# Reordered waits in a two-layer hybrid trunk: gate scans, attention scores, filler jobs and their evictions change places

## The chip, the core and the metric

The kernel runs on one core of a Trainium2 chip. The metric is device time of one execution in microseconds (us). Engines are named TensorE (PE), VectorE (DVE), ScalarE (ACT), GpSimd (POOL) and SyncE (SP).

## What is computed

Two trunk layers are applied to a prompt of 128 tokens and to a sample of 256 tokens with cached context, at width 1024, in float32. The reference, cut to what matters:

```python
h = rms_norm(x, norm1_w) * (1 + scale1) + shift1
(mq, mk, mv, mo, mg, nq, nk, nv, dq, dk, dv, sz, sxbc, sdt, gpre) = split_cols(h @ w_in)   # 1024 x 7448
a_out = mlstm_mixer(...)      # gated linear attention, forward and backward
b_out = na_mixer(...)         # neighbourhood attention, 4 heads
c_out = diff_mixer(...)       # p0 - lam * p1 from two softmaxes, 4 heads
d_out = ssm_mixer(...)        # 5-tap convolution, then a decaying scan, forward and backward
gates = sigmoid(gpre)         # 4 x 1024 columns
mixed = sum(gates * (branches @ w_branch))
x = x + gate1 * (mixed @ w_out)
x = x + gate2 * expert_choice_ffn(rms_norm(x, norm2_w) * (1 + scale2) + shift2, ...)       # 16 experts
```

## The kernel before, in words

The 384 tokens are three tiles (TT) of 128. Each layer has the same stages, written out by hand engine by engine, with semaphores between them. Each engine works its own list in order, so an instruction that waits holds up all that stand behind it.

1. **Projections.** Seven weight tiles (PROJ_TILES) are multiplied in three passes: each weight quarter is split by ACT (high_parts: rounding copy into a four-slot ring, line 1368) and by POOL (low_parts: difference, line 710), and PE does 24 matmuls per quarter (three_passes, line 769). Between them PE turns the gate rows: line 871 waits for rows_ready, which DVE signals after the gate scans (lines 1860 to 1872). DVE does, in this order: norm of the neighbourhood queries and keys (nan_ready), the 20 steps of the convolution (lines 1843, 1845, conv_ready), the gate scans (rows_ready).
2. **Filler jobs.** The 32 gate quarters (g0 to g31; 24 matmuls each), the 8 modulation partials (p0 to p7; 16 matmuls, line 775) and their sums (s0 to s7; 8 matmuls, line 781) are 48 jobs in the order JOB_ORDER. PE runs them between the small matmuls of the mixers. They alternate between banks 0 and 1: a job waits until the one two before it is evicted by take_job on ACT (line 1513, tanh, or 1368, copy). take_job also starts a store of the previous gate and then splits weights of later quarters (high_parts(AHEAD[j])).
3. **Neighbourhood attention** (ten units). PE: a job, na_scores(i), na_turn(i-1), na_out(i-2). DVE: na_in (scale, bias, maximum), na_take. ACT: na_exp (waits for o_evac of unit i-2, since the sum SSUM has two places), take_job, na_turned.
4. **Differential attention** (twelve units). PE: df_scores(i), a job, df_turn(i-1), df_out(i-2). DVE: df_max(i), df_mix(i-1), df_take(i-2). After the last df_out DVE normalises the result (head_norm) and only then turns to the decays.
5. **Two decay scans** (decays(0) for the mLSTM, decays(1) for the SSM), 8 combinations c each. PE: decay_row(c) (line 1065), jobs at c = 1 to 6, and scan_scores (lines 1055 to 1057), which in scan 0 at c = 2, 4, 6 waits for pm_ready of the first c combinations and in scan 1 at c = 4 for four. DVE: exponent(c) (line 2048 on), then scored(c-1) (lines 2063 to 2069, pm_ready). ACT (combos): the exponential of c (line 1584, waits for e_ready), then, from c = 1, take_job. One job more follows each scan on PE. Then come the numerators (line 1086).
6. **Branches.** Five jobs, the transposes of the branch results (line 1157), a wait for their split and for all jobs, then 8 column blocks of the branch matmuls, the output projection, the second norm and the router.
7. **Experts.** 96 weight halves of 2 MB each stream from memory.

Of the kernel before, what the change touches and what calls it, by code (L numbers as in the profile page):

```python
# [29 lines left out]
TT = 3  # L30
# [40 lines left out]
def constants():  # L71
# [31 lines left out]
    for g in range(4):  # L103
        for r in range(2):
# [13 lines left out]
JOB_ORDER = ("g0 p0 g1 s0", "g2 g3 p1 g4 s1 g5 p2 g6 s2 g7", "g8 g9 g10 g11 g12 g13 g14 g15 g16 g17 g18 g19",  # L118
             "p3 g20 s3 g21 p4 s4 g22", "p5 g23", "g24 s5 p6 g25 s6 g26 g27", "g28 p7 g29 s7 g30 g31")
# [137 lines left out]
def trunk_program(nc, dr, outs):  # L257

    (y_prompt, y_sample, new_na_k, new_na_v, new_diff_k, new_diff_v, new_C, new_n, new_m, new_ssm) = outs
    with ExitStack() as ctx:  # L260
# [224 lines left out]
        SSUM = st([2, 2])  # L485
# [3 lines left out]
        DREC = st([2, 2])  # L489
        WPT = st([TT, 16])  # L490
# [267 lines left out]
        def _(pe):  # L758
# [57 lines left out]
            for l in range(L):  # L816
# [181 lines left out]
                pe.wait_ge(sem["dfn_ready"], l + 1)  # L998
                pe.wait_ge(sem["s_read"], 10 * (l + 1))
                for t in range(TT):  # L1000
                    for c in range(4):
                        mm = pe.transpose(PS[:, 2 + t, c * 128:(c + 1) * 128], DQK[:, t, c * 128:(c + 1) * 128], ident)
                    mm.then_inc(sem["dtr_out"], 1)
                dunits = [(t, h) for t in range(TT) for h in range(4)]

                def df_scores(u):
                    t, h = dunits[u]
                    if u >= 2:
                        pe.wait_ge(sem["d_exp"], 12 * l + u - 1)
                    else:  # L1010
                        pe.wait_ge(sem["dtr_evac"], 3 * (l + 1))
# [31 lines left out]
                for i in range(14):  # L1043
                    if i < 12:
                        df_scores(i)
                        job()
                    if 1 <= i <= 12:
                        df_turn(i - 1)
                    if i >= 2:
                        df_out(i - 2)  # L1050


# [93 lines left out]
                for _ in range(5):  # L1146
# [6 lines left out]
                for g in range(6):  # L1153
# [4 lines left out]
                    mm.then_inc(sem["brt_out"], 1)  # L1158
                pe.wait_ge(sem["brt_evac"], 6 * (l + 1))
                pe.wait_ge(sem["brt_lo"], 6 * (l + 1))  # L1160
                pe.wait_ge(sem["job_evac"], NJ * (l + 1))
                for dc in range(8):
                    if dc >= 2:
                        pe.wait_ge(sem["bp_evac"], 8 * l + dc - 1)
                    w = next_quarter()
                    for nb in range(4):
                        hi, lo_ = w[nb // 2]
                        for k in range(2):
                            kk = 2 * (nb % 2) + k
                            mm = three_passes(PS[:, 4 * (dc % 2) + nb, 0:T], (hi[:, kk, :], lo_[:, kk, :]),  # L1170
# [3 lines left out]
                for dcs in ((0, 1), (2,), (3,), (4,), (5,), (6,), (7,)):  # L1174
# [5 lines left out]
                    for k in range(KC):  # L1180
                        if dcs[0] == 0:
                            pe.wait_ge(sem["mixl_ready"], 8 * l + k + 1)
                        for dc in dcs:
                            hi, lo_ = w[dc]
                            mm = three_passes(PS[:, 2 + dc % 4, 0:T], (hi[:, k, :], lo_[:, k, :]), (MIXH[:, k, :], MIX[:, k, :]), k == 0, k == KC - 1)
# [180 lines left out]
        def _(act):  # L1366
# [47 lines left out]
            for l in range(L):  # L1414
# [85 lines left out]
                def take_job():  # L1500
# [18 lines left out]
                    high_parts(AHEAD[j])  # L1519
# [13 lines left out]
                def na_exp(u):  # L1533
                    act.wait_ge(sem["s_read"], 10 * l + u + 1)
                    if u < 2:
                        for c in range(2):
                            ins = act.activation(ED[:, u, c * 128:(c + 1) * 128], ED[:, 2 + u, c * 128:(c + 1) * 128], ACT.Exp,
                                                 bias=SMX[:, u, c:c + 1], accum_out=SSUM[:, u, c:c + 1])
                    else:
                        ins = act.activation(ED[:, u % 2, :], ED[:, 2 + u % 2, :], ACT.Exp, bias=SMX[:, u % 2, 0:1], accum_out=SSUM[:, u % 2, 0:1])  # L1540
# [32 lines left out]
                for i in range(13):  # L1573
                    if i < 12:
                        df_exp(i)
                        take_job()
                    if i >= 1:
                        df_turned(i - 1)

                def combos(kind):  # L1580
                    for c in range(8):
# [3 lines left out]
                        if c:  # L1585
                            take_job()

                combos(0)
# [8 lines left out]
                combos(1)  # L1597
# [3 lines left out]
                for _ in range(5):  # L1601
                    take_job()
                for g in range(6):
                    t, half = g // 2, g % 2
                    act.wait_ge(sem["brt_out"], 6 * l + g + 1)
                    copy(rounded(BRT[:, 4 * half:4 * half + 4, t * 128:(t + 1) * 128]), PS[:, 2 + g, :].rearrange("p (a b) -> p a b", a=4)).then_inc(sem["brt_evac"], 1)

# [102 lines left out]
        def _(dve):  # L1710
# [34 lines left out]
            for l in range(L):  # L1745
# [91 lines left out]
                dve.wait_ge(sem["proj_evac"], l * N_PROJ + 11)  # L1837
                for c in range(4):
                    for jj in range(5):
                        wv = CP("conv_w")[:, 5 * c + jj:5 * c + jj + 1]  # L1840
                        src = XB[:, c, jj:jj + 388]
                        if jj == 0:
                            ins = TS(CV[:, c, 2:390], src, wv, CP("conv_b")[:, c:c + 1], ALU.mult, ALU.add)
                        else:
                            ins = STT(CV[:, c, 2:390], src, wv, CV[:, c, 2:390], ALU.mult, ALU.add)  # L1845
                        if jj < 4:
                            ins.then_inc(dve_step, 1)
                            dve.wait_ge(dve_step, step())
                ins.then_inc(sem["conv_ready"], 1)
                dve.wait_ge(sem["conv_ready"], l + 1)  # L1850


# [24 lines left out]
                TTo(MOUT[64:68, 1:2], ROWS[64:68, 2, 0:1], ROWS[64:68, 0, 0:1], ALU.subtract).then_inc(sem["m_out"], 1)  # L1877

# [456 lines left out]
```

## Time and profile before

| | us |
|---|---|
| median of 3 runs | 2066.54 |
| lowest and highest run | 2056.85, 2066.82 |
| the profiled execution | 2068.15 |
| its span, first to last instruction | 2066.4 |
| PE busy | 1793.6 (87%) |
| DVE, ACT, POOL busy | 645.3, 548.3, 518.7 |
| DMA: bytes moved | 567.76 MB |

The span covers all but 1.75 us of the profiled execution. A PE matmul is recorded with its latency and overlaps its neighbours, so the busy share says little about its pace; starts of matmuls and idle times do. The clock granted to TensorE is 1.2 or 2.4 GHz; rows give it as a share of 2.4.

### The profile page before, as it was taken

How to read it: one execution, taken by the hardware profiler on the slowest of the kernel's cores; microseconds unless marked ns; L12 is line 12 of the kernel's file. 1: busy time of each engine (PE TensorE's matmuls, PEld its weight loads, DVE VectorE, ACT ScalarE, POOL GpSimd, SP SyncE). 2: the span in 40 equal slices, each digit the busy share in tenths (PEclk: the TensorE clock that was granted, in tenths of full speed). 3: DMA queues.
4: the chain of work that ended last, by engine and by line, in shares of the span. 5: the costliest groups of instructions: out<-in, count | busy, mean ns of one | idle time of the engine just before them, and what ended most of it. 6: DMA issues, size and time to landing. Idle time of an engine off the chain costs nothing.

```text
span 2066.4 us, 22539 instructions
## 1 busy us (share of the span) xinstructions
PE 1793.6 (87%) x9096; PEld 1138.6 (55%) x9096; DVE 645.3 (31%) x1349; ACT 548.3 (27%) x1054; POOL 518.7 (25%) x654
## 2 busy tenths in 40 slices
PE   5989999999899788878879899999996987888787
PEld 2878897789553222222248788967882422222223
DVE  2185245647310001001144642556653000000111
ACT  3433343222431111101144333522224211110111
POOL 0785343148200000000037652523561000000000
PEclk8999898999999999999989998989998999999999
DMA  9524533455589999999973253335544999999996
GB/s 350 138 102 138 181 105 117 175 165 207 207 360 426 426 427 426 428 426 427 427 210 123 79 206 111 113 138 172 194 177 170 389 427 428 426 428 426 427 426 265
DMA packets 123543, 567.76 MB, mean 275 GB/s; under 512 B 21808, under 2 KB 31280, under 8 KB 98352
## 3 DMA queue, kind: packets, MB, share of 16 engines
q1 hardware_dynamic: 112656, 543.91, 66.5%
q10 hardware_dynamic: 9920, 20.84, 2.8%
q0 software_dynamic: 864, 1.58, 0.3%
q8 instruction: 72, 1.18, 0.2%
q14 instruction: 31, 0.25, 0.0%
HBM read 550.57 MB, written 15.73 MB: 274 GB/s over the span
## 4 chain that ended last, share of the span: by engine, by line
PE 49%; DMA 33%; DVE 9%; POOL 4%; ACT 3%; issue 1%; SPq 1%; ACTq 0%; DVEq 0%
PE banks L769 22%; PE banks L1269 11%; DMA ring<-in_w_up 9%; DMA ring<-in_w_gate 7%; DMA ring<-in_w_down 6%; DMA work<-in_w_gate 4%; POOL ring_fp32r L710 3%; DMA work<-in_w_up 3%; PE banks L775 2%; DMA ring<-in_w_ada 2%; DVE work L1845 2%; DMA work<-in_w_down 1%; PE banks L1086 1%; PE banks L1065 1%; ACT work L1368 1%; PE banks L1239 1%
## 5 line engine op out<-in xcount | busy, mean ns | idle before, releaser
L710 POOL TENSOR_TENSOR ring_fp32r<-ring,ring_fp32r 128x256 fp32r<-128x256 f32 x592 | 467.2, 822 | 912.4 <-ACT ring_fp32r L1368 911.9
L1269 PE MATMUL banks<-ring,work 128*64 128x512 f32 x1776 | 402.6, 597 | 74.9 <-DMA ring<-in_w_gate 33.3
L769 PE MATMUL banks<-xT_fp32r,ring_fp32r 128*128 128x384 f32 x1280 | 356.0, 351 | 1.6 <-POOL ring_fp32r L710 1.6
L1368 ACT ACTIVATE work<-banks 32x512 f32<-32x512 f32 (+7 forms) x404 | 205.7, 528 | 487.3 <-PE banks L1269 250.8
L1269 PEld LDWEIGHTS banks<-ring,work 128*64 128x64 f32 x1776 | 122.4, 136 | 333.2 <-issue 198.8
L1269 PE MATMUL banks<-work 128*64 128x512 f32 x972 | 225.8, 601 | 42.8 <-DMA work<-in_w_gate 15.1
L769 PEld LDWEIGHTS banks<-xT_fp32r,ring_fp32r 128*128 128x128 f32 x1280 | 241.3, 195 | 10.6 <-issue 3.6
L769 PE MATMUL banks<-hT_fp32r,ring_fp32r 128*128 128x384 f32 x640 | 219.4, 343 | 0.0
L1368 ACT ACTIVATE ring_fp32r<-ring 128x1024 fp32r<-128x1024 f32 (+1 forms) x164 | 154.8, 970 | 158.2 <-PE banks L769 126.8
L2247 DVE SCALAR_TENSOR_TENSOR xT<-banks,mod,xT 128x128 f32<-128x128 f32 (+1 forms) x128 | 47.0, 413 | 446.3 <-PE banks L1305 446.0
L1269 PEld LDWEIGHTS banks<-work 128*64 128x64 f32 x972 | 67.7, 137 | 182.9 <-issue 112.4
L769 PE MATMUL banks<-work_fp32r,ring_fp32r 128*128 128x384 f32 x768 | 146.1, 350 | 15.5 <-issue 8.7
L769 PEld LDWEIGHTS banks<-work_fp32r,ring_fp32r 128*128 128x128 f32 x768 | 138.6, 194 | 21.2 <-issue 11.0
L1661 ACT ACTIVATE work<-banks 128x512 f32<-128x512 f32 x32 | 19.1, 598 | 483.3 <-PE banks L1269 483.3
L769 PE MATMUL banks<-ring_fp32r,xT_fp32r 128*128 128x512 f32 (+1 forms) x480 | 137.8, 373 | 1.2 <-DVE small L1791 1.2
L769 PEld LDWEIGHTS banks<-hT_fp32r,ring_fp32r 128*128 128x128 f32 x640 | 124.6, 195 | 2.6 <-issue 1.2
L2269 DVE TENSOR_TENSOR work<-work,banks 128x512 f32<-128x512 f32 x32 | 22.0, 688 | 293.0 <-PE banks L1269 292.9
L769 PEld LDWEIGHTS banks<-ring_fp32r,xT_fp32r 128*128 128x128 f32 x480 | 87.9, 191 | 16.4 <-DVE small L1791 1.4
L1269 PE MATMUL banks<-hT,work 128*64 128x512 f32 x324 | 75.2, 599 | 20.6 <-DMA work<-in_w_gate 8.3
L769 PE MATMUL banks<-ring_fp32r,hT_fp32r 128*128 128x512 f32 (+1 forms) x240 | 89.1, 371 | 0.0
L775 PE MATMUL banks<-ring,c 128*32 128x512 f32 x384 | 59.1, 745 | 20.8 <-DMA ring<-in_w_ada 10.6
L1513 ACT ACTIVATE work<-banks 128x384 f32<-128x384 f32 x64 | 31.1, 486 | 141.6 <-PE banks L769 141.6
(287 smaller groups left out, 1687.3 us busy)
## 6 DMA issues: line engine op xcount, KB each, us to landing
ring<-in_w_up SPq DMA_DIRECT2D x38, 2048.0 KB, 30.6
ring<-in_w_gate SPq DMA_DIRECT2D x37, 2048.0 KB, 30.5
ring<-in_w_down SPq DMA_DIRECT2D x36, 2048.0 KB, 30.3
ring<-in_w_in SPq DMA_DIRECT2D x28, 2048.0 KB, 8.4
ring<-in_w_ada SPq DMA_DIRECT2D x24, 2048.0 KB, 8.5
work<-in_w_down SPq DMA_DIRECT2D x20, 2048.0 KB, 30.6
work<-in_w_gate SPq DMA_DIRECT2D x18, 2048.0 KB, 30.5
work<-in_w_up SPq DMA_DIRECT2D x16, 2048.0 KB, 30.6
```

Source lines behind the costliest of these rows:

```text
L710: ins = pool.tensor_tensor(rounded(w_), w_, rounded(hi_), ALU.subtract)
L769: mm = pe.matmul(dst, a_, b_, start=(first and i == 0), stop=(last and i == 2))
L775: mm = pe.matmul(PS[32 * g:32 * g + 32, bank, :], c32[:, k, :], w[:, k, :], start=(k < 4), stop=(k >= 4), tile_position=(0, 32 * g))
L1065: pe.matmul(PS[:, 4 + c % 4, 0:T], ident[:, r:r + 1].broadcast_to([128, 128]), ROWS[:, 0, :], start=True, stop=True)\
L1086: mm = pe.matmul(dst, PM[:, 2 * h + d, off:off + 128], v(d, ks), start=(i == 0), stop=(i == len(pairs) - 1))
L1239: mm = pe.matmul(dst, rounded(strided(part[:, t, 512 * (q // 8):512 * (q // 8) + 512], q // 2 % 4)), rounded(SEL[:, t, a:b, :].rearrange(" ...
L1269: mm = pe.matmul(dst[64 * hf:64 * hf + 64, :], x(k), w[kk][:, 512 * hf:512 * hf + 512], start=(k == 0), stop=(k == KC - 1), tile_position= ...
L1368: return act.activation(dst, src, ACT.Copy, scale=scale)
L1513: ins = act.activation(GATES[:, i % 8, :], PS[:, job_bank(j), 0:T], ACT.Tanh, scale=0.5)
L1845: ins = STT(CV[:, c, 2:390], src, wv, CV[:, c, 2:390], ALU.mult, ALU.add)
L2247: ins = STT(xT[:, dc, a:b], PS[:, bank, a:b], mod[:, 40 + dc, g:g + 1], xT[:, dc, a:b], ALU.mult, ALU.add)
L2269: TTo(HH[:, e % 2, :], SA, PS[:, 2 * (e % 2) + 1, :], ALU.mult).then_inc(sem["hh_ready"], 1)
```

## The change

- The gate scans stand ahead of the convolution on DVE.
- The jobs' order changes at the start: g0, g1, p0, g2, s0 instead of g0, p0, g1, s0, g2. JOB_SITES says where each job stands; the neighbourhood loop has s0 as its first job instead of g2.
- The neighbourhood loop on PE issues scores(i) ahead of the job. The exponential's sum has four places (NSUM), so na_exp(i) waits for o_evac of unit i-4. ACT splits weights after na_turned instead of before it; the same in the differential loop.
- The transposes of the differential queries and keys stand among the last two neighbourhood outputs, and the first scores need two of the three evictions.
- DVE's df_take stands one unit later and ahead of df_mix. The last df_turn and df_out leave the loop; df_out(11) stands behind decay_row(1) and the job p3.
- In combos two jobs are evicted before the first exponential; the tuple says how many follow each one.
- The last job, g31, moves behind the transposes of the branches. The wait for all jobs stands at the second column block, and banks of the branch and output matmuls are swapped to allow it.

```diff
-JOB_ORDER = ("g0 p0 g1 s0", "g2 g3 p1 g4 s1 g5 p2 g6 s2 g7", "g8 g9 g10 g11 g12 g13 g14 g15 g16 g17 g18 g19",
-             "p3 g20 s3 g21 p4 s4 g22", "p5 g23", "g24 s5 p6 g25 s6 g26 g27", "g28 p7 g29 s7 g30 g31")
+JOB_SITES = (("xs", "g0"), ("nq", "g1"), ("na_in", "p0 g2"),
+             ("na", "s0"), ("na", "g3"), ("na", "p1"), ("na", "g4"), ("na", "s1"), ("na", "g5"), ("na", "p2"), ("na", "g6"), ("na", "s2"), ("na", "g7"),
...
+             ("scan0", "p3 g20 s3 g21 p4 s4 g22"), ("state0", "p5 g23"), ("scan1", "g24 s5 p6 g25 s6 g26 g27"), ("state1", "g28"),
+             ("tail", "p7 g29 s7 g30"), ("branch", "g31"))
...
# PE
-                for i in range(12):
-                    if i < 10:
+                for i in range(10):
+                    na_scores(i)
+                    for _ in range(NA_JOBS[i]):
                         job()
-                        na_scores(i)
-                    if 1 <= i <= 10:
+                    if i >= 1:
                         na_turn(i - 1)
                     if i >= 2:
                         na_out(i - 2)
...
+                na_turn(9)
+                pe.wait_ge(sem["dfn_ready"], l + 1)
+                pe.wait_ge(sem["s_read"], 10 * (l + 1))
+                df_transposes(0)
+                df_transposes(1)
+                na_out(8)
+                df_transposes(2)
+                na_out(9)
...
+                df_turn(11)
+                df_out(10)
                 pe.wait_ge(sem["d_exp"], 12 * (l + 1))
-                pe.wait_ge(sem["do_evac"], 12 * (l + 1))
                 for c in range(8):
                     decay_row(0, c)
                     if 1 <= c <= 6:
                         job()
+                    if c == 1:
+                        df_out(11)
+                        pe.wait_ge(sem["do_evac"], 12 * (l + 1))
...
-                for _ in range(5):
+                for _ in range(4):
                     job()
...
+                job()
                 pe.wait_ge(sem["brt_evac"], 6 * (l + 1))
                 pe.wait_ge(sem["brt_lo"], 6 * (l + 1))
-                pe.wait_ge(sem["job_evac"], NJ * (l + 1))
                 for dc in range(8):
+                    if dc == 1:
+                        pe.wait_ge(sem["job_evac"], NJ * (l + 1))
...
# ACT
-                        if i >= 2:
-                            act.wait_ge(sem["o_evac"], 10 * l + i - 1)
+                        if i >= 4:
+                            act.wait_ge(sem["o_evac"], 10 * l + i - 3)
                         na_exp(i)
-                        take_job()
+                        for _ in range(NA_JOBS[i]):
+                            take_job(False)
                     if i >= 1:
                         na_turned(i - 1)
+                    high_parts(AHEAD[jobs[0] - 1])
...
+                def combos(kind, taken):
+                    for _ in range(taken[0]):
+                        take_job()
                     for c in range(8):
                         act.wait_ge(sem["e_ready"], 16 * l + 8 * kind + c + 1)
...
-                        if c:
+                        for _ in range(taken[c + 1]):
                             take_job()
-                combos(0)
+                combos(0, (2, 0, 1, 1, 1, 1, 0, 1, 0))
...
-                combos(1)
+                combos(1, (2, 1, 1, 0, 1, 1, 0, 1, 0))
...
# DVE
-                for i in range(14):
+                for i in range(15):
                     if i < 12:
                         df_max(i)
+                    if i >= 3:
+                        df_take(i - 3)
                     if 1 <= i <= 12:
                         df_mix(i - 1)
-                    if i >= 2:
-                        df_take(i - 2)
```

The block from the wait for growT to m_out moves, unchanged, from behind conv_ready to ahead of the convolution.

## Rows read from the trace of the kernel before

**Rows 1.** The page's 40 slices: granted TensorE clock and DMA share, in tenths.

```profile
PEclk8999898999999999999989998989998999999999
DMA  9524533455589999999973253335544999999996
```

**Rows 2.** Waits of PE, 0 to 560 us: total us, times, longest us.

```profile
PE banks L769 <- issue: 4.4, 1, 4.4
PE banks L775 <- ACT work L1513: 2.9, 1, 2.9
PE banks L1030 <- DVE work L1996: 2.6, 1, 2.6
PE banks L985 <- ACT work L1368: 2.0, 2, 1.2
PE banks L969 <- ACT work L1540: 1.3, 1, 1.3
```

**Rows 3.** DVE in order of time, convolution and gate scans: start us, us.

```profile
124.78 0.89 DVE L1843 TENSOR_SCALAR work<-work,colp 128x388 f32<-128x388 f32 x1
...
144.39 2.02 DVE L1860 TENSOR_TENSOR_SCAN work<-banks,cst 64x128 f32<-64x128 f32 x4
...
149.21 0.72 DVE L1872 TENSOR_TENSOR_SCAN work<-work,small 4x256 f32<-4x256 f32 x1
...
170.57 1.76 DVE L1900 TENSOR_TENSOR work<-work 128x1536 f32<-128x1536 f32 x1 [12.24 <-ACT work L1368]
```

**Rows 4.** PE in order of time, around the turned gate rows and the first partial job.

```profile
149.98 2.18 PE L871 MATMUL banks<-cst,work 128*128 128x128 f32 x9 [6.92 <-DVE work L1872]
...
186.28 1.92 PE L775 MATMUL banks<-ring,c 128*32 128x512 f32 x16 [2.48 <-DMA ring<-in_w_ada]
```

**Rows 5.** One window: length, busy us (count) per engine, PEclk, DMA share, GB/s.

```profile
152.20:155.60 3.40, 3.40 (x11) 2.65 (x11) 0.68 (x7) 3.26 (x11) 0.00 (x0) 0.63 0.00 0
```

**Rows 6.** Chain that ended last: two gate jobs of the neighbourhood loop.

```profile
218.69 6.27 PE banks L769 x24
...
230.82 4.25 PE banks L769 x24
```

**Rows 7.** PE in order of time, end of the differential loop and scan 0.

```profile
334.25 1.51 PE L1040 MATMUL banks<-work 128*128 128x64 f32 x6 [0.41 <-DVE work L2001]
...
350.57 0.48 PE L1055 MATMUL banks<-work 64*128 64x128 f32 x2
...
360.52 1.92 PE L775 MATMUL banks<-ring,c 128*32 128x512 f32 x16
...
365.10 0.48 PE L1055 MATMUL banks<-work 64*128 64x128 f32 x2 [0.82 <-DVE work L2069]
```

**Rows 8.** DVE in order of time: last take, first exponent, end of the second scored.

```profile
335.79 0.22 DVE L2001 COPY work<-banks 128x64 f32<-128x64 f32 x1 [1.70 <-PE banks L1040]
...
343.62 0.35 DVE L2048 SCALAR_TENSOR_TENSOR work<-banks,work,cst 128x128 f32<-128x128 f32 x1
...
347.81 0.42 DVE L2069 TENSOR_TENSOR work<-work,banks 128x256 f32<-128x256 f32 x1
```

**Rows 9.** ACT in order of time: eviction of g21, split, exponential.

```profile
358.50 0.49 ACT L1513 ACTIVATE work<-banks 128x384 f32<-128x384 f32 x1 [2.21 <-PE banks L769]
358.89 1.05 ACT L1368 ACTIVATE ring_fp32r<-ring 128x1024 fp32r<-128x1024 f32 x1
361.66 0.63 ACT L1584 ACTIVATE work<-work 128x512 f32<-128x512 f32 x1 [1.73 <-DVE work L2054]
```

**Rows 10.** PE in order of time, scan 1.

```profile
401.53 3.64 PE L775 MATMUL banks<-ring,c 128*32 128x512 f32 x16 [2.93 <-ACT work L1513]
...
411.16 0.49 PE L1055 MATMUL banks<-work 64*128 64x128 f32 x2
```

**Rows 11.** Chain that ended last, entry to the branch matmuls.

```profile
460.29 6.74 PE banks L769 x24
...
468.28 4.06 POOL ring_fp32r L710 x4
```

More of the change, by code:

```diff
@@ L115 @@
 PROJ_TILES = ((C_MQ, 512, 4), (C_NQ, 512, 7), (C_XBC, 512, 11), (C_MV, 512, 14), (C_NV, 512, 17), (C_DK, 512, 20), (C_SZ, 256, 23))
-JOB_ORDER = ("g0 p0 g1 s0", "g2 g3 p1 g4 s1 g5 p2 g6 s2 g7", "g8 g9 g10 g11 g12 g13 g14 g15 g16 g17 g18 g19",
-             "p3 g20 s3 g21 p4 s4 g22", "p5 g23", "g24 s5 p6 g25 s6 g26 g27", "g28 p7 g29 s7 g30 g31")
+JOB_SITES = (("xs", "g0"), ("nq", "g1"), ("na_in", "p0 g2"),
[5 rows of a table added]
+JOB_ORDER = tuple(_s[1] for _s in JOB_SITES)
+NA_JOBS = [len(_s[1].split()) for _s in JOB_SITES if _s[0] == "na"]
+DF_JOBS = [len(_s[1].split()) for _s in JOB_SITES if _s[0] == "df"]
 JOBS = [({"g": "gate", "p": "part", "s": "sum"}[_w[0]], int(_w[1:])) for _part in JOB_ORDER for _w in _part.split()]
@@ L484, in trunk_program @@
         SMX = st([2, 2])
-        SSUM = st([2, 2])
         SREC = st([2, 2])
@@ L489, in trunk_program @@
         DREC = st([2, 2])
+        NSUM = small[:, sm[0] - 12:sm[0] - 4].rearrange("p (a b) -> p a b", a=4)
         WPT = st([TT, 16])
@@ L995, in _, with df_transposes @@
                         na_out(i - 2)
-                pe.wait_ge(sem["dfn_ready"], l + 1)
-                pe.wait_ge(sem["s_read"], 10 * (l + 1))
-                for t in range(TT):
+                def df_transposes(t):
                     for c in range(4):
@@ L1010, in df_scores @@
                     else:
-                        pe.wait_ge(sem["dtr_evac"], 3 * (l + 1))
+                        pe.wait_ge(sem["dtr_evac"], 3 * l + 2 + u)
                     for mp in range(2):
@@ L1041, in df_out @@
                     mm.then_inc(sem["do_out"], 1)
-                for i in range(14):
-                    if i < 12:
-                        df_scores(i)
+                for i in range(12):
+                    df_scores(i)
+                    for _ in range(DF_JOBS[i]):
                         job()
-                    if 1 <= i <= 12:
+                    if i >= 1:
                         df_turn(i - 1)
@@ L1498, in _, with take_job @@
                 jobs = [0]
-                def take_job():
+                def take_job(split=True):
                     j = jobs[0]
@@ L1518, in take_job @@
                         act.dma_start(spill[l, g % 8, :, g // 8, :], GATES[:, g % 8, :]).then_inc(spilled[g % 8], 16)
-                    high_parts(AHEAD[j])
+                    if split:
+                        high_parts(AHEAD[j])
                 take_job()
@@ L1575, in _ @@
                         df_exp(i)
-                        take_job()
+                        for _ in range(DF_JOBS[i]):
+                            take_job(False)
                     if i >= 1:
                         df_turned(i - 1)
-                def combos(kind):
+                    high_parts(AHEAD[jobs[0] - 1])
+                def combos(kind, taken):
+                    for _ in range(taken[0]):
+                        take_job()
                     for c in range(8):
@@ L1600, in _ @@
                 copy(SS_OUT[0:64, :, :], PS[0:64, 3, :].rearrange("p (a b) -> p a b", a=8)).then_inc(sem["st_evac"], 1)
-                for _ in range(5):
+                for _ in range(4):
                     take_job()
@@ L1835, in _ @@
                 ins.then_inc(sem["nan_ready"], 1)
[L1837 to L1850, printed above, removed]
                 dve.wait_ge(sem["growT"], l + 1)
@@ L1877, in _ @@
                 TTo(MOUT[64:68, 1:2], ROWS[64:68, 2, 0:1], ROWS[64:68, 0, 0:1], ALU.subtract).then_inc(sem["m_out"], 1)
+                dve.wait_ge(sem["proj_evac"], l * N_PROJ + 11)
+                for c in range(4):
+                    for jj in range(5):
+                        wv = CP("conv_w")[:, 5 * c + jj:5 * c + jj + 1]
+                        src = XB[:, c, jj:jj + 388]
+                        if jj == 0:
+                            ins = TS(CV[:, c, 2:390], src, wv, CP("conv_b")[:, c:c + 1], ALU.mult, ALU.add)
+                        else:
+                            ins = STT(CV[:, c, 2:390], src, wv, CV[:, c, 2:390], ALU.mult, ALU.add)
+                        if jj < 4:
+                            ins.then_inc(dve_step, 1)
+                            dve.wait_ge(dve_step, step())
+                ins.then_inc(sem["conv_ready"], 1)
+                dve.wait_ge(sem["conv_ready"], l + 1)
                 dve.wait_ge(sem["tm_evac"], l + 1)
```

16 lines of the change are left out of this document (8 added, 8 removed), and 2 rows, old and new, of the table JOB_SITES.

## The prediction

> **What bounds the kernel now.** I read the page's slices first. The DMA engines are full in slices 12 to 20 and 32 to 40, and TensorE's clock is at its upper level there [rows 1]: the experts stream their weights, and nothing in the change touches them. Their stream starts when the stage ahead of it lets go of buffers, so a microsecond won or lost in the mixers moves the end by one. The mixers are two stretches (layer 0 up to about 560 us, layer 1 from about 1040 to 1590 us) with DMA mostly below half and a clock that dips [rows 1]. There PE is the engine to watch.
>
> Then the waits of PE, which show how little of the mixers is idle, and who ends it: ACT ends 2.0 and 1.3 us in the neighbourhood loop, DVE 2.6 us at the last df_turn, ACT 2.9 us at the partial p6, "issue" 4.4 us ahead of the branch matmuls [rows 2], DVE 6.92 us at the turned gate rows and a DMA 2.48 us at p0 [rows 4]. Last, the clock: the 24 matmuls of a gate job take 4.25 us in the one row and 6.27 us in the other [rows 6]; the long one stands behind a stretch of small matmuls. At 1.2 GHz a job costs up to twice its time, and low clock follows idle or thin work. So each wait has a price beside its length. The chain names PE for nearly all of the neighbourhood stage and for both scans, so times are summed on PE, per layer; both layers run the same list.
>
> **What the change saves, per layer.**
>
> *Gate scans.* DVE starts the convolution at 124.78, reaches the scans at 144.39 and ends them at 149.93; PE takes the rows at 149.98 [rows 3, 4]. Put first, the scans need growT, which PE gives near 127, so they end near 132.5, long before PE comes (143.1, that is 149.98 less the wait). The wait goes: 6.9. The nine transposes took 2.18 us at low clock, about 1.1 less at full clock, and the following window stood at 0.63 [rows 4, 5], which is (1 - 0.63) x 3.4 = 1.3 lost, with a little of the window ahead 1.5. Sum 9.5. Price: the convolution ends at 132.8 + 19.6 = 152.4, eight later than before. Behind it wait ACT's tanh and, behind those on ACT, the splits for the last projection tile; they come at about 155 to 157, POOL's part of 3 to 4 us ends by 160.7, and PE, now early, wants the first of them at 160.2. It fits within half a microsecond. DVE had 12.24 us of slack at line 1900 [rows 3], so its next work is not late. I take the cost as 0 (bound 1).
>
> *Job order.* p0 waits 2.48 us for its weights [rows 4]; g1, some 4.3 us, now stands ahead of it. SP still issues that load at the end of the last projection. The load that follows p0 starts one gate job later and is wanted four jobs on, about 12 us against some 8 us in flight: hidden. Saved: 2.5.
>
> *Neighbourhood loop.* With scores(i) ahead of the job, DVE's maximum and ACT's exponential have the job to hide behind, and na_turn finds them done even where the job is a sum of 1 us. With four sums ACT no longer waits for the output of unit i-2. The waits of 2.0 and 1.3 us, with 0.7 at the first df_scores, go: 4.0. The low clock beside them: three gate jobs of this stage took 6.3 to 6.7 us instead of 4.25 (the long row is one of the three) [rows 6], about 6.5 us, and the small matmuls in the same stretches some 3.5 more, 10 together. It isn't sure to come back, because the stretches of small matmuls around the sums keep their content, and the first of them lost the clock with no wait in it. Bounds 0 and 10; I take 5.
>
> *g31 behind the branch transposes.* The gap of 4.4 us is filled, and the first column block ran 6.74 us where 4.2 is the pace [rows 2, 11]. What counts is when POOL starts its run of splits, 468.28, since the branch stage goes at POOL's pace of about 5 us per block from there. ACT evicts g31 and splits two more quarters after it (2.7 us), POOL takes two parts of 2.8 to 4 us, so POOL's run starts at about 4.8 earlier. The loads of xT and of w_out wait for g31 as well and stay ahead of their use by tens of microseconds. Saved 4.8 (bounds 3.5 and 6).
>
> Sum of gains: 9.5 + 2.5 + 4.0 + 5.0 + 4.8 = 25.8 us per layer.
>
> **What it costs, per layer.**
>
> *df_out(11) behind p3.* The wait of 2.6 us at df_turn(11) stays: df_mix(11) still stands behind df_take(9), and that behind df_out(9). Before, df_out(11) ended near 335.7 and DVE took it at 335.79; 7.8 us of norm later came the first exponent (343.62), and pm_ready for two combinations at 348.23, 12.4 us after the take [rows 7, 8]. PE wanted it at 350.57 and had 2.3 us in hand. Now two rows, one set of scores and p3 come ahead of df_out(11). At the low clock seen there these are 1.6 + 2.5 + 1.6 + 3.6 = 9.3 us, less 0.4 of wait: the take moves to 344.7, pm_ready to 356.9. PE has row and g20 left and is through with them at 350.3. It then idles 6.6 us and goes on 6.4 later than before. At full clock the same count gives 6.7 idle. Cost 6.4.
>
> *Evictions ahead of exponentials, scan 0.* The tuple makes ACT wait for g21 ahead of exponential 3, for s4 ahead of 5 and for g22 ahead of 7. But scan_scores at c = 4 waits for pm_ready of four, which needs exponential 3, while PE does g21 first. From the end of g21: eviction 0.46, split 1.05, exponential 0.63 [rows 9], DVE's scored about 0.9, latencies 0.2, that is 3.2 us in which PE is idle, where before there was no wait. The same 3.2 behind g22 ahead of the numerators. Behind s4 it is about 2.65, where 0.82 stood [rows 7]: 1.8 more. Cost 8.2.
>
> *Scan 1.* g24 and s5 are evicted ahead of the exponentials, so p6 doesn't wait (2.93) and runs at full clock (1.92 instead of 3.64) [rows 7, 10]; with the row and part of g25 behind it, g25 ends 5.3 earlier. Then come its eviction and split (1.5), exponential 2 (0.8 with the hand-over), scored(2), exponent(4), scored(3) (2.8): 5.1 idle, and the scores start where they started before, at 411.2. g27 is again evicted ahead of exponential 7: 3.2 idle less 0.2. Cost 3.0.
>
> Waits alone: 6.4 + 8.2 + 3.0 = 17.6.
>
> *The clock in these waits.* The gaps of 6.6 and 5.1 us are longer than the 2.6 and 2.9 us after which the profile shows half clock (3.64 us for the partials behind each). After the first, scores, row, sum and row run slow (2.8 more) and g21 in part (about 2); after the second, scores and two rows (2) and g26 in part (2); behind g21 and s4 up to 2.7; behind g22 and g27 up to 1.5 each. All of it is 14.5, none of it is 0. I take 11, since idle of this length did cost the clock each time here. Costs: 28.6 us per layer.
>
> df_take one unit later, the swapped banks and the two-of-three eviction wait cost nothing: the takes are hidden under PE's gate jobs.
>
> **The sum.** 25.8 - 28.6 = -2.8 per layer, 5.6 us lost in two. 2068.15 + 5.6 = 2073.8 in the terms of the profiled execution, which lies 1.6 above the median of the runs: 2072.
>
> **A rule weighed.** The gaps on PE [rows 2, 4] are all ones that the edits aim at. The Trainium skill (Perfetto Trace Analysis, Optimization Strategy) says to find the gaps on the contended engine and to make the dependencies that end them start sooner. By that rule alone only gains are counted, which is the last rival below; against it stands that here the same in-order lists move other dependencies later.
>
> **Rivals.**
> - *Slower: the clock decides.* The neighbourhood stretches lose it as before (gain 5 becomes 0) and every new gap pays in full (14.5). 20.8 - 32.1 = -11.3 per layer: 2089. For it: the first of these stretches fell with no wait in it. It decides once the new gaps cost over 13 while the loop wins under 3. Chance 0.35.
> - *Faster: the clock holds in the new gaps.* 25.8 - 17.6 = 8.2 per layer: 2050. For it: most new gaps are 3.2 us or less; against it: 2.6 and 2.9 us were enough before. Chance 0.20.
> - *Only gains.* DVE's and ACT's chains in the scans have slack that I don't see, and p6's 2.9 is saved too: 28.7 per layer, 2009. Against it: the slack was 2.3 us where 9 is asked. Chance 0.08.
> - *The forecast*, gains and losses cancel within 0.5%: 0.37.
>
> 0.5% (10 us) is about what a measurement of this kernel can tell from no change. Faster 0.28, same 0.37, slower 0.35. The forecast's own range is 2057 to 2077; to hold 8 in 10, the range takes in both clock rivals with their slack: 2042 to 2094.
>
> **What the changed profile would show.** Right: no wait of PE on the scans at the turned gate rows; none on a DMA at p0; none on ACT in the neighbourhood loop; branch matmuls directly behind g31. A wait of PE of 6 to 7 us at the scores of scan 0 (lines of scan_scores) ended by DVE, three more there of 2.5 to 3.3, and in scan 1 one near 5 and one near 3. Wrong: if those are absent, the time falls towards 2010 to 2050; if the last projection tile waits for POOL, the convolution's delay costs after all; if gate jobs around the sums of the neighbourhood loop take 4.3 us throughout, its clock gain is 10 and not 5.

## The result, and the profile after

Changed kernel: median 2093.95 us (2089.19 to 2099.04, 4 runs). Kernel before, on the same chip: 2062.59 us (2056.85 to 2066.82, 4 runs). The ratio is 1.0155, 95% interval [1.0122, 1.0188]: slower by 1.5%. Forecast were 2072 us and a range that ended at 2094. The profiled execution took 2094.4 us, 26.2 more in span than the one before.

The page of the changed kernel: span, and of the 40 slices the granted clock and the DMA share.

```profile
span 2092.6 us, 22533 instructions
...
PEclk8999997779989999999999999978898999999999
DMA  9536332325599999999973353414453999999996
```

The experts' stream (DMA at 9) fills the same slices as before [rows 1], with a span that is 26 us longer. Three slices in a row, 7 to 9 (314 to 471 us), stand at clock 7: they are scan 0, scan 1 and the numerators behind each in layer 0.

Waits of PE in layer 0, 0 to 600 us, after:

```profile
PE banks L1066 <- DVE work L2094: 16.6, 4, 7.0
...
PE banks L1101 <- DVE work L2094: 5.8, 2, 2.9
...
PE banks L776 <- DVE work L2216: 3.1, 4, 1.8
PE banks L1043 <- DVE work L2021: 2.1, 1, 2.1
```

Of the waits in [rows 2], those of the gate rows on DVE (6.92), of p0 on its DMA (2.48), of the neighbourhood loop on ACT, of p6 (2.9) and the "issue" ahead of the branches are gone. In their place PE waits 16.6 us at the scores of the scans (L1066 is the first line of scan_scores) and 5.8 us ahead of the numerators (L1101), both ended by scored on DVE (L2094). The wait at the last df_turn (L1043) is 2.1 where 2.6 stood. The short ones on DVE in the branch stage (L2216) are 3.1 in four, where the kernel before had 1.6 in three at the same step (its L2191):

```profile
PE banks L769 <- DVE work L2191: 1.6, 3, 0.6
```

The new waits in order of time on PE:

```profile
331.14 0.79 PE L1066 MATMUL banks<-work 64*128 64x128 f32 x2 [6.96 <-DVE work L2094]
...
346.92 0.49 PE L1066 MATMUL banks<-work 64*128 64x128 f32 x2 [2.89 <-DVE work L2094]
...
356.52 0.79 PE L1066 MATMUL banks<-work 64*128 64x128 f32 x2 [2.07 <-DVE work L2094]
...
368.44 4.89 PE L1101 MATMUL banks<-work 128*128 128x65 f32 x24 [2.89 <-DVE work L2094]
...
374.10 3.52 PE L1101 MATMUL banks<-work 128*128 128x65 f32 x16
...
415.64 0.79 PE L1066 MATMUL banks<-work 64*128 64x128 f32 x2 [4.71 <-DVE work L2094]
...
436.64 8.24 PE L1101 MATMUL banks<-work 128*128 128x64 f32 x40 [2.89 <-DVE work L2094]
```

Predicted were 6.6, 3.2, 2.65, 3.2, 5.1 and 3.2. Every wait is there, in its place and nearly at its size. The 2.89 is made of the chain on ACT and DVE between the end of a gate job and the numerators. ACT after the change:

```profile
365.59 0.49 ACT L1530 ACTIVATE work<-banks 128x384 f32<-128x384 f32 x1 [9.18 <-PE banks L776]
365.98 1.05 ACT L1385 ACTIVATE ring_fp32r<-ring 128x1024 fp32r<-128x1024 f32 x1
366.93 0.62 ACT L1608 ACTIVATE work<-work 128x512 f32<-128x512 f32 x1
```

and DVE:

```profile
367.98 0.41 DVE L2094 TENSOR_TENSOR work<-work,banks 128x256 f32<-128x256 f32 x1
```

ACT has stood idle for 9.18 us for g22 (PE L776), evicts it, splits a quarter, and only then makes the last exponential; scored ends at 368.4 and PE starts.

What was not foreseen is the price behind it. Windows of the changed kernel over five stages of layer 0 (length, busy us and count per engine, PEclk, DMA share, GB/s): the neighbourhood loop, scan 0, numerators 0, scan 1, numerators 1 up to the branches.

```profile
180.00:236.00 56.00, 56.00 (x372) 48.74 (x370) 23.98 (x60) 26.16 (x60) 24.91 (x33) 1.00 0.53 186
308.80:368.40 59.60, 44.52 (x168) 29.24 (x167) 21.46 (x69) 11.31 (x20) 9.94 (x15) 0.72 0.29 100
368.40:394.80 26.40, 26.36 (x139) 22.98 (x140) 12.42 (x26) 1.86 (x4) 1.49 (x3) 0.61 0.15 51
394.80:436.60 41.80, 34.24 (x157) 27.57 (x155) 20.82 (x63) 12.28 (x21) 15.80 (x22) 0.84 0.42 141
...
436.60:470.00 33.40, 33.36 (x185) 30.05 (x186) 15.08 (x42) 2.35 (x5) 2.20 (x4) 0.74 0.33 119
```

The same five stages of the kernel before:

```profile
196.00:260.00 64.00, 59.90 (x326) 51.65 (x325) 15.69 (x51) 21.82 (x53) 22.27 (x34) 0.84 0.45 158
336.20:372.90 36.70, 35.88 (x161) 24.16 (x162) 20.57 (x67) 9.14 (x16) 5.62 (x8) 0.82 0.38 132
372.90:389.30 16.40, 16.40 (x139) 14.72 (x138) 10.46 (x24) 4.15 (x7) 2.79 (x4) 1.00 0.25 78
389.30:423.70 34.40, 31.47 (x158) 24.37 (x157) 22.38 (x65) 11.41 (x19) 13.74 (x20) 0.90 0.46 162
...
423.70:453.20 29.50, 29.50 (x211) 26.91 (x210) 15.22 (x42) 6.36 (x12) 6.08 (x9) 1.00 0.51 148
```

The neighbourhood loop won clock: 0.84 to 1.00 in layer 0, 0.86 to 0.93 in layer 1. Both stages of numerators lost theirs with PE busy throughout: 1.00 to 0.61 and 1.00 to 0.74. The same 139 records take 16.4 us before and 26.4 after. Inside the first of them:

```profile
370.00:389.00 19.00, 19.00 (x90) 16.07 (x89) 6.86 (x18) 0.00 (x0) 0.00 (x0) 0.50 0.00 1
```

A clock of 0.50 is the lower level, 1.2 GHz. These 19 us of back-to-back matmuls run on it. Before, the same work ran at the upper one:

```profile
376.50:380.00 3.50, 3.50 (x34) 3.50 (x33) 1.41 (x4) 0.00 (x0) 0.88 (x2) 1.00 0.02 5
```

**Layer 0 stage by stage**, from the start of the first instruction of each stage on PE:

| Stage | before us | after us | difference |
|---|---|---|---|
| TM turn to end of last projection | 52.5 | 43.1 | -9.4 |
| to g8 (job order, neighbourhood loop) | 81.3 | 64.6 | -16.7 |
| to the first row of scan 0 (df loop) | 76.5 | 71.8 | -4.7 |
| scan 0 | 36.7 | 59.6 | +22.9 |
| numerators 0 | 16.4 | 26.4 | +9.9 |
| scan 1 | 34.4 | 41.9 | +7.4 |
| numerators 1, state, last jobs (g31 left out of both) | 25.2 | 33.3 | +8.1 |
| branches to output projection, with g31's 4.2 in both | 59.1 | 55.8 | -3.3 |
| sum | 382.1 | 396.5 | +14.4 |

Layer 1 goes from 380.8 to 393.6, +12.8. With 3.4 lost ahead of the TM turn, where nothing was changed (first loads of the kernel), and 4.4 won in the two expert stretches, these make 26.2: the whole difference.

### The profile page after: what moved, and what is told of

Read it like the earlier page. It is cut to its first block, busy times and chain, and to the rows that moved or that the text cites. A ratio compares the mean times of both kernels' runs of the same rounds, so it can differ in the third digit from the quotient of the medians.

```text
span 2092.6 us, 22533 instructions
## 1 busy us (share of the span) xinstructions
PE 1814.2 (87%) x9096; PEld 1161.0 (55%) x9096; DVE 645.6 (31%) x1349; ACT 547.1 (26%) x1054; POOL 522.4 (25%) x654
## 4 chain that ended last, share of the span: by engine, by line
PE 55%; DMA 33%; DVE 4%; POOL 4%; ACT 2%; SPq 1%; issue 1%; ACTq 0%; DVEq 0%
PE banks L776 26%; PE banks L1286 11%; DMA ring<-in_w_up 9%; DMA ring<-in_w_gate 7%; DMA ring<-in_w_down 6%; DMA work<-in_w_gate 4%; DMA work<-in_w_up 3%; POOL ring_fp32r L717 3%; PE banks L1101 3%; PE banks L782 2%; PE banks L1076 1%; DMA work<-in_w_down 1%; DMA ring<-in_w_ada 1%; PE banks L788 1%; PE banks L1256 1%; ACT work L1385 1%
## 5 line engine op out<-in xcount | busy, mean ns | idle before, releaser
L776 PE MATMUL banks<-xT_fp32r,ring_fp32r 128*128 128x384 f32 x1280 | 360.1, 354 | 1.8 <-POOL ring_fp32r L717 1.8
L776 PEld LDWEIGHTS banks<-xT_fp32r,ring_fp32r 128*128 128x128 f32 x1280 | 244.2, 197 | 14.0 <-issue 6.2
L776 PE MATMUL banks<-hT_fp32r,ring_fp32r 128*128 128x384 f32 x640 | 221.7, 346 | 0.0
L2272 DVE SCALAR_TENSOR_TENSOR xT<-banks,mod,xT 128x128 f32<-128x128 f32 (+1 forms) x128 | 46.7, 412 | 444.7 <-PE banks L1322 444.4
L776 PE MATMUL banks<-work_fp32r,ring_fp32r 128*128 128x384 f32 x768 | 145.1, 347 | 10.7 <-DVE work L2216 6.9
L776 PEld LDWEIGHTS banks<-work_fp32r,ring_fp32r 128*128 128x128 f32 x768 | 137.1, 192 | 17.1 <-DVE work L2216 7.5
L776 PE MATMUL banks<-ring_fp32r,xT_fp32r 128*128 128x512 f32 (+1 forms) x480 | 136.3, 369 | 1.2 <-DVE small L1816 1.2
L776 PEld LDWEIGHTS banks<-hT_fp32r,ring_fp32r 128*128 128x128 f32 x640 | 125.9, 197 | 2.8 <-issue 1.7
L776 PEld LDWEIGHTS banks<-ring_fp32r,xT_fp32r 128*128 128x128 f32 x480 | 86.7, 189 | 16.0 <-DVE small L1816 1.4
L776 PE MATMUL banks<-ring_fp32r,hT_fp32r 128*128 128x512 f32 (+1 forms) x240 | 88.4, 368 | 0.0
L782 PE MATMUL banks<-ring,c 128*32 128x512 f32 x384 | 56.2, 713 | 11.5 <-DMA ring<-in_w_ada 7.1
```

Of the source, the lines that this page charges most:

```text
L776: mm = pe.matmul(dst, a_, b_, start=(first and i == 0), stop=(last and i == 2))
L782: mm = pe.matmul(PS[32 * g:32 * g + 32, bank, :], c32[:, k, :], w[:, k, :], start=(k < 4), stop=(k >= 4), tile_position=(0, 32 * g))
L2272: ins = STT(xT[:, dc, a:b], PS[:, bank, a:b], mod[:, 40 + dc, g:g + 1], xT[:, dc, a:b], ALU.mult, ALU.add)
```

## The experiments

Each is given as median, range and number of runs, and the ratio to the kernel before on the same chip with its 95% interval. "tuples" are the second arguments of combos(0, ...) and combos(1, ...); the first number is how many jobs ACT evicts ahead of the first exponential, the others how many behind each one.

**1. The gate scans alone.** The kernel before, with the block from the wait for growT to m_out ahead of the convolution.

```diff
+                dve.wait_ge(sem["growT"], l + 1)
+                segs = ...        (the block up to m_out, unchanged)
                 dve.wait_ge(sem["proj_evac"], l * N_PROJ + 11)
```

> The kernel before with one edit, the gate scans ahead of the convolution. Theory: the edit wins the wait of 6.9 us at the turned gate rows and the low clock behind it, 9 us per layer, and the convolution's later end costs nothing: 2062.6 - 18 = 2045 us, with PE's first matmul of the last projection tile directly behind the tile ahead of it. Rival: the later splits on ACT and POOL hold PE up by a few us per layer, so that under 10 us in all is won (2053 or more).

2048.64 us (2045.3 to 2049.84, 4), ratio 0.9915 [0.9884, 0.9946]. PE's wait on the gate scans is gone from its waits, no other took its place. This term and its size hold.

**2. The changed kernel, last exponential ahead of the last job.**

```diff
-                combos(0, (2, 0, 1, 1, 1, 1, 0, 1, 0))
+                combos(0, (2, 0, 1, 1, 1, 1, 0, 0, 1))
-                combos(1, (2, 1, 1, 0, 1, 1, 0, 1, 0))
+                combos(1, (2, 1, 1, 0, 1, 1, 0, 0, 1))
```

> The changed kernel with one edit: the last job of each scan (g22, g27) is evicted behind the last exponential instead of ahead of it, tuples (2,0,1,1,1,1,0,0,1) and (2,1,1,0,1,1,0,0,1). It takes away only the two waits of 2.9 us ahead of the numerators in each layer. Theory (a short wait also costs the clock, and the numerators run at half clock behind it, 17 us instead of 9): 2.9 + 7 to 8 us per scan, 40 us in all, 2094 - 40 = 2054. Rival (a wait costs its length): 4 x 2.9 = 12 us, 2082.

2052.96 us (2045.19 to 2061.14, 10), ratio 0.9937 [0.9913, 0.9961]: 41 us less than the changed kernel by the medians, with two numbers changed in each tuple. The waits of PE ahead of the numerators and at the scores, layer 0:

```profile
PE banks L1066 <- DVE work L2094: 16.7, 4, 7.0
...
PE banks L1101 <- DVE work L2094: 0.7, 1, 0.7
```

and the numerators on PE:

```profile
365.24 2.79 PE L1101 MATMUL banks<-work 128*128 128x65 f32 x24
...
368.37 1.90 PE L1101 MATMUL banks<-work 128*128 128x65 f32 x16
```

The waits at the scores are what they were (16.7). Only 5.8 - 0.7 = 5.1 us of waiting per layer went, 10 in two layers; the other 31 us are clock: 16 matmuls in 1.90 us, where the changed kernel took 3.52. The rival, that a wait of this kind costs its own length, would have had 2082.

**3. The changed kernel, df_out(11) back ahead of the rows.**

```diff
                 df_out(10)
+                df_out(11)
                 pe.wait_ge(sem["d_exp"], 12 * (l + 1))
+                pe.wait_ge(sem["do_evac"], 12 * (l + 1))
...
-                    if c == 1:
-                        df_out(11)
-                        pe.wait_ge(sem["do_evac"], 12 * (l + 1))
```

> The changed kernel with one edit: df_out(11) stands ahead of the decay rows again, and the wait for do_evac with it; the eviction tuples stay. Theory: the wait of 7.0 us at the first c = 2 scores goes to about 0, and with it part of the low clock behind it: 7 to 10 us per layer, 2094 - 17 = 2077 (2073 to 2080). Rival: DVE's norm chain isn't what sets it, and the wait moves to the next scores: no more than 3 us per layer, 2088.

2096.7 us (2095.99 to 2102.11, 4), ratio 1.0156 [1.0123, 1.0189]: nothing won. My theory missed. PE at the first scores of scan 0:

```profile
331.14 0.48 PE L1066 MATMUL banks<-work 64*128 64x128 f32 x2 [3.77 <-DVE work L2093]
```

The wait is 3.77 instead of 6.96, but it isn't gone: a second cause stands behind the first. With 2 as the first number of the tuple, ACT evicts p3 and g20 ahead of exponential 0, and scores at c = 2 need exponentials 0 and 1. ACT shows it:

```profile
327.41 0.49 ACT L1529 ACTIVATE work<-banks 128x384 f32<-128x384 f32 x1 [4.37 <-PE banks L776]
327.79 1.14 ACT L1607 ACTIVATE work<-work 128x512 f32<-128x512 f32 x2
```

It idles 4.37 us for g20, and both exponentials come only behind that eviction. That the scores start at 331.14 in both kernels is chance, since g8, the first job of the differential loop, starts at 237.0 in the changed kernel and at 240.1 here. Counted from g8 they start after 94.1 us in layer 0 and 89.2 in layer 1 of the changed kernel, and after 91.0 and 89.8 here. The prediction priced the early evictions only behind g21, s4 and g22. Runs 9 and 10 part the two causes.

**4. The changed kernel with df_out(11) and the evictions back.** As 3, and both tuples (0, 0, 1, 1, 1, 1, 1, 1, 1), which is the order of the kernel before. What stays of the change is the gate scans, the job order, the neighbourhood loop and g31.

> The changed kernel with df_out(11) back and both eviction tuples as before the change (0,0,1,1,1,1,1,1,1); all else is the change's. Theory: every wait that the change put into the scans is gone, and with them their low clock; the rest is gain: per layer 9 (gate scans), 16 (neighbourhood stage), 3 (tail), so 2062.6 - 56 = 2007, between 2000 and 2020. Rival: these gains depend on each other or are given back at the scans, whose DVE chain now comes too early or too late: 2035 or more.

2007.39 us (2004.85 to 2010.56, 4), ratio 0.9723 [0.9686, 0.976]. Waits of PE in layer 0, where 16.6 and 5.8 stood:

```profile
PE banks L1066 <- DVE work L2093: 0.8, 1, 0.8
...
PE banks L782 <- ACT work L1529: 2.9, 1, 2.9
```

and the numerators at the upper level:

```profile
349.54 2.79 PE L1100 MATMUL banks<-work 128*128 128x65 f32 x24
...
352.66 1.90 PE L1100 MATMUL banks<-work 128*128 128x65 f32 x16
```

This measures all the gains at once: (2068.25 - 2007.39) / 2 = 30.4 us per layer against the 25.8 predicted. The difference to the changed kernel, 0.0432 of some 2065 us, is 44.6 per layer, against 28.6 predicted for the costs.

**5. As 4, with the two early evictions in scan 1 alone,** tuple (2, 0, 0, 0, 1, 1, 1, 1, 1) there.

> As the kernel with df_out(11) and the evictions of before, but in scan 1 the jobs g24 and s5 are evicted ahead of the first exponential and the others stay behind theirs, tuple (2,0,0,0,1,1,1,1,1). Theory: p6 still waits for nothing ahead of it (it needs g24 only), so the wait of 2.9 us and the half clock behind it go: 4 to 6 us per layer, 8 to 12 less than its sister kernel, near 1997. Rival: the wait moves to s6 or to the scores, and the two kernels are level.

2001.07 us (1992.63 to 2007.18, 4), ratio 0.9724 [0.9659, 0.9789], level with 4 in the ratio. p6's wait of 2.9 us is gone. Of the two at the scores, 0.8 is the old one of scan 0 and 1.2 is new:

```profile
PE banks L1066 <- DVE work L2093: 2.0, 2, 1.2
```

The trace does show a gain in scan 1, which takes 29.9 us at clock 1.00 in both layers, where run 4 has 33.2 and 34.2:

```profile
361.40:391.30 29.90, 28.68 (x157) 23.47 (x157) 22.38 (x65) 11.30 (x19) 13.66 (x20) 1.00 0.53 186
```

These 3 to 4 us per layer are too little for the ratio to tell. The wait of 4.7 us isn't there: the two early evictions alone don't make it. The changed kernel's tuple also evicts p6 and g25 ahead of exponential 2, and this one doesn't.

**6. The kernel before, with the tuples of the changed kernel alone.**

> The kernel before with the change's eviction tuples and nothing else. Theory: the waits behind g21, s4, g22, g25 and g27 appear here too (2.9, 2.1, 2.9, 4.7, 2.9) with half clock at the numerators; per layer 8 us of waits in scan 0, 3 net in scan 1 and 15 or more of clock: 2062.6 + 2 x 26 = 2115 (2105 to 2125). Rival: they hurt only behind the late df_out(11), and cost 2062.6 + 10 at most.

2148.97 us (2144.09 to 2153.07, 4), ratio 1.0431 [1.0375, 1.0487]. The direction holds, the size doesn't: +89 us, where +47 was expected. Its waits in layer 0 show the same four gaps at the scores as run 3 (3.77, 2.89, 2.07, 4.71) and the two of 2.89 at the numerators, beside the old one at the gate rows:

```profile
PE banks L1055 <- DVE work L2071: 13.4, 4, 4.7
...
PE banks L871 <- DVE work L1874: 6.9, 1, 6.9
PE banks L1086 <- DVE work L2071: 5.8, 2, 2.9
```

(13.4 + 5.8) less the 0.8 and 2.9 that the order before has is 15.5 per layer, 31 in two. The remaining 58 us are in no wait of PE. Much of it is the clock at the numerators, here in windows of layer 0 (numerators 0, then numerators 1 up to the branches):

```profile
386.70:411.40 24.70, 24.64 (x138) 22.44 (x139) 11.12 (x25) 1.87 (x4) 1.49 (x3) 0.65 0.15 51
...
452.60:491.60 39.00, 38.92 (x208) 35.63 (x209) 14.88 (x43) 4.92 (x10) 4.48 (x8) 0.74 0.28 102
```

The kernel before takes 16.4 and 29.5 us for them at clock 1.00. That is 18 per layer, 36 in two. The two scans of layer 0 take 22.5 us longer, 15.5 of it waits and 7 of it clock. Some 8 us of the 89 are not placed.

**7. The changed kernel, jobs ahead of the scores in the neighbourhood loop.**

```diff
                 for i in range(10):
-                    na_scores(i)
                     for _ in range(NA_JOBS[i]):
                         job()
+                    na_scores(i)
```

> The changed kernel with one edit: in the neighbourhood loop PE does the job ahead of the scores again. Theory (scores first is what closes the waits and keeps the clock): waits of 1 to 2 us by ACT come back at some of ten units and the clock falls, 4 to 8 us per layer, 2094 + 12 = 2106. Rival (the four sums and the order of ACT do it, and the place of the scores is worth nothing): 2094 within 5 us.

2099.49 us (2095.11 to 2108.91, 4), ratio 1.0198 [1.0138, 1.0258]; the interval overlaps that of the changed kernel. One wait of the loop comes back:

```profile
PE banks L976 <- ACT work L1558: 1.0, 1, 1.0
```

The clock of the loop stays at 1.00 in layer 0 and 0.93 in layer 1, as in the changed kernel. So the place of the scores isn't what gave the loop its clock.

**8. The changed kernel, g31 back ahead of the branch transposes** (five jobs instead of four behind the last scan, none behind the transposes, on PE and ACT).

> The changed kernel with one edit: g31 stands ahead of the branch transposes again. Theory: the gap of 4.4 us with half clock behind it comes back, 3 us per layer: 2100. Rival: behind g31 the gate loads come too late, a new wait of DVE on them takes all that is won, and the time stays at 2094 or falls.

2102.45 us (2099.78 to 2103.89, 4), ratio 1.0205 [1.0152, 1.0258]. The gap is back:

```profile
PE banks L776 <- issue: 4.4, 1, 4.4
```

The direction is the theory's, but the interval overlaps that of the changed kernel, so this run by itself doesn't show a gain of g31's place. The stage times above do (3.3 in layer 0).

**9. As 4, with df_out(11) late alone.** Tuples as before, df_out(11) at c = 1.

> The kernel with df_out(11) and the evictions of before (2007.4 us), with one edit of the change put back: df_out(11) behind decay_row(1) and p3. Theory (my count of DVE's norm chain): a wait of 6 to 7 us by DVE at the first c = 2 scores comes back, with half clock behind it: 8 to 11 us per layer, 2007 + 19 = 2026. Rival (the earlier experiment, in which undoing it won nothing): 2007 to 2012.

2027.2 us (2025.63 to 2028.8, 4), ratio 0.9821 [0.9792, 0.985]: 20 us more than in 4.

```profile
330.76 0.79 PE L1066 MATMUL banks<-work 64*128 64x128 f32 x2 [6.96 <-DVE work L2094]
```

**10. As 4, with the two early evictions in scan 0 alone.** Tuple (2, 0, 0, 0, 1, 1, 1, 1, 1) in combos(0, ...).

> The kernel with df_out(11) and the evictions of before, with one part of the tuple put back: in scan 0 p3 and g20 are evicted ahead of exponential 0, all others stay behind theirs. Theory: exponential 0 waits for g20, and PE then for about 3.8 us at the c = 2 scores (the wait that stayed when only df_out(11) was undone), with half clock behind it: 5 to 8 us per layer, 2007 + 13 = 2020. Rival: without the other evictions the wait is taken up by the following jobs, 2007 within 5.

2026.59 us (2017.56 to 2029.68, 4), ratio 0.9808 [0.9775, 0.9842]: 19 us more than in 4.

```profile
330.85 0.48 PE L1066 MATMUL banks<-work 64*128 64x128 f32 x2 [3.77 <-DVE work L2093]
```

Without either cause (run 4) the scores at c = 2 start 87.3 us after g8 in layer 0 and 87.5 in layer 1. The late df_out(11) alone makes it 92.5 in both, the early evictions alone 91.2 and 91.3, and each alone costs 10 us per layer. Together, in the changed kernel, it is 94.1 and 89.2, on average 91.7 and so no later than with the late output alone. That is why 3 won nothing: two causes that end at nearly the same moment hide each other, and taking one back shows little of either.

**11. As 4, jobs ahead of the scores in the neighbourhood loop.** The edit of 7 on 4.

> The kernel with df_out(11) and the evictions of before, with the job ahead of the scores in the neighbourhood loop. Theory after the sister experiment: the four sums and ACT's order close the waits, the scores' place is worth one wait of 1 us per layer: 2009. Rival: the scores' place keeps the clock up, and without it some stretch falls to half clock: 2014 or more.

2009.95 us (2005.23 to 2014.1, 4), ratio 0.9734 [0.9705, 0.9763]: level with 4. The place of the scores is worth about 1 us per layer at most.

**12. As 4, with the last job of both scans evicted ahead of exponential 7.** Both tuples (0, 0, 1, 1, 1, 1, 1, 2, 0): the opposite of 2.

> The kernel with df_out(11) and the evictions of before, with only the last job of each scan (g22, g27) evicted ahead of exponential 7, as in the change: (0,0,1,1,1,1,1,2,0) for both. It puts a single wait of 2.9 us ahead of the numerators, four in all, into a kernel with no other new wait. Theory (the wait sets off half clock in the numerators whatever stood before): four times 2.9 + 7 to 8, 2007 + 40 = 2047. Rival (it was the sum of several waits that brought the clock down): 2007 + 12 = 2019.

2053.11 us (2049.43 to 2055.09, 5), ratio 0.9942 [0.992, 0.9963]: 46 us more than in 4, from the eviction of one job moved ahead in each scan.

```profile
350.16 4.82 PE L1100 MATMUL banks<-work 128*128 128x65 f32 x24 [2.89 <-DVE work L2093]
355.74 3.51 PE L1100 MATMUL banks<-work 128*128 128x65 f32 x16
```

Four waits of 2.89 us in two layers are 11.6 us. The other 34, or 8.6 behind each wait, are the clock, in accord with the 9.9 and 8.1 of the stage table and with the 31 us of run 2.

All 14 traces together say the same. They hold 56 stages of numerators. The 24 that stand behind a wait of 2.89 us all lose clock (24.7 or 26.3 us instead of 16.4 behind scan 0). The 30 without a wait all run at 1.00. Two, in run 2, stand behind 0.70 us: one keeps the clock, and the other loses it on the way (25.4 and 31.7 us, up to the branches).

## Why the prediction was wrong

The path was right and the sum was not. By the parts of the prediction, per layer:

**Gate scans, 9.5.** In the traces 9.4 in layer 0, 8.7 in layer 1, and 9 by run 1 (0.85% of 2065 in two layers). The convolution's delay cost nothing, as argued.

**Job order and neighbourhood loop, 2.5 + 4.0 + 5.0.** Measured 16.7 up to g8. The 5.0 for the clock was the middle of 0 to 10, and layer 0 reached the upper end: all gate jobs of the loop take 4.4 us, and the loop runs at clock 1.00. Layer 1 got 14.6, with a clock of 0.93. Over all traces the stretch takes 80.9 us with the old loop (6 layers) and 66.9 with the changed one (18 layers), that is 14 won, some 7.5 of it clock. I had doubted it because the first slow stretch showed no wait. It went in layer 0 all the same. It isn't the place of the scores (runs 7 and 11); which of the job order, the fourth sum and the order on ACT did it was not parted.

**g31, 4.8.** Measured 3.3. The "issue" gap and the slow first column block are gone, but a load that had been hidden is now in the chain that ended last, as it shows for the stretch:

```profile
472.75 4.18 PE banks L776 x24
477.28 8.30 DMA work<-gates_spill
491.13 3.97 POOL ring_fp32r L717 x4
```

**df_out(11) behind p3, 6.4.** The wait of 6.96 came as worked out (6.6; the working's own take at 344.7 and its 12.4 us give 6.8), and alone this edit costs 10 us per layer with its clock (run 9). But beside the early evictions it costs nothing more (run 3). The prediction missed that the first number of the tuple holds exponential 0 behind g20.

**Evictions, waits 8.2 + 3.0.** The waits of 2.89, 2.07, 2.89, 4.71 and 2.89 stand where 3.2, 2.65, 3.2, 5.1 and 3.2 were put. With the wait of df_out(11), they add 14.0 us of idle to scan 0 (14.8 less the old 0.82) and 4.7 to scan 1 (7.6 less p6's 2.93): 18.7, against 17.6 predicted for waits alone.

**The clock in the new waits, 11 (at most 14.5): the step that failed.** Run 4 has the changed kernel's list without the moved output and evictions, so it is the one to compare with. From g8 to the branch transposes it takes 186.2 us in layer 0 and 185.8 in layer 1, the changed kernel 232.9 and 226.2: 46.7 and 40.4 more. Its waits of PE there sum to 6.7, those of the changed kernel to 24.9, which is 18.2 in each layer. The rest, 28.5 and 22.2, some 25 us per layer, goes with the low clock: more than twice the value taken and 10 over its bound. Most of it is one item, "behind g22 and g27 up to 1.5 each": the stage table has 9.9 and 8.1 for it in layer 0. The other items together had 11.5 of the bound and came to some 7. I had priced a fall of the clock by the few matmuls that stand behind it, as [rows 10] show for the partials, and taken for granted, without a row for it, that a dense stretch comes back at once. The numerators are dense, and didn't.

Together: gains of 30 per layer where 25.8 were predicted, costs of 44 where 28.6 were. The rival "the clock decides" named the mechanism and its side, and had 2089; its terms are not those measured either, since it gave the neighbourhood loop no clock and the numerators 3 us.

The rival "only gains" had 2009. The Trainium skill (Perfetto Trace Analysis, Optimization Strategy) says to find the gaps on the contended engine and start sooner what ends them. Run 4, which keeps the edits that close gaps and leaves out those that move evictions and an output to where they open new ones, has 2007. The agreement to 2 us is in part luck: 2009 counts the 2.9 us of p6, which run 4 still waits for, and only 5.0 for the loop's clock. The trace of the changed kernel shows what the rule leaves uncounted, the gaps that a reordered queue opens elsewhere.

**Still open.** Why the numerators stay at the lower level for most of a stage when a wait of 2.89 us stands ahead of them, and hold the upper one when none does (2.79 us for 24 matmuls against 4.82), is told by no run. A run with wider matmuls ahead of them was not made. A version without p6's wait and without the new ones was not found: run 5 came nearest. Of all versions measured, 4 and 5 are the best, 2.8% below the kernel before, with run 11 level.

## What to carry to other kernels

When work moves forward in an in-order queue, ask what it waits for itself, and which step behind it now waits too. Here an eviction stood ahead of an exponential and waited for its job to end, so the exponential did, and then PE did. Price a new gap on PE by the clock of the whole stage that follows, not by the gap or the next few matmuls: 2.9 us ahead of a stage of small matmuls cost 10 to 11.5 (runs 2 and 12). And when undoing one edit changes nothing, look whether another cause ends the wait at nearly the same moment before calling the edit free. Count such moments from a common mark, not from the start of the run.

## What the runs showed of the hardware

- A stretch of matmuls 128x65, back to back and with PE busy at 100%, stayed at a granted clock of 0.50 for 19 us (370 to 389 us of the changed kernel, with a few other small matmuls and one partial at its end) behind a wait of 2.89 us. The same stretch without a wait ran at 1.00 throughout (16 matmuls in 1.90 us against 3.52).
- A single such wait is enough: in run 12 it is the only new one ahead of the numerators, and their 16 matmuls take 3.51 us.
- The neighbourhood loop, with the same small matmuls, ran at 0.84 to 0.88 in the 6 layers with the old order and at 0.93 to 1.00 in the 22 with the changed one, where waits of 2.0 and 1.3 us are gone and the jobs are reordered.
